# An expert layer on one Trainium2 core: 128 tokens by fetched rows instead of 64, the dense part 384 wide instead of 448

## The chip, the cores and the metric

The kernel runs on one core of a Trainium2 chip, as one program launched once. The metric is the time on the device in microseconds (us). Five engines of the core appear: TensorE (PE, with its weight loads as PEld), VectorE (DVE), ScalarE (ACT), GpSimd (POOL) and SyncE (SP), which here only issues DMAs. All DMAs of the core share 16 DMA engines.

## The reference, cut to what matters

Two transformer blocks run over 512 tokens of width 1024. The first block has sliding-window attention (blocks of 128 tokens; the first block has no block before it, so its masked scores against it become zero weights), a pooling branch, and then an expert layer with 16384 experts. Only these two parts are touched:

```python
kp = jnp.pad(k, ((0,0),(BLOCK,0),(0,0),(0,0)))          # zeros ahead of the first block
mask = (rel >= 0) & (rel < WINDOW) & (kpos[None, :] >= 0)
sc = jnp.where(mask, sc, NEG_INF)                       # softmax over window and sink
...
idx = jnp.take_along_axis(cidx, fi, axis=-1)            # 8 heads x 16 experts for each token
g = jax.nn.softmax(fv, axis=-1)
a = jax.nn.gelu(jnp.einsum('chkd,cd->chk', u_tab[idx], xc))
y = jnp.einsum('chk,chkd->cd', g * a, v_tab[idx])
```

The second block (a recurrent mixer, a feed-forward layer, an embedding gate) is the same before and after.

## The kernel before

Tensors lie with their 1024 channels in 8 chunks of 128 partitions and the 512 tokens along the free dimension. Every large product is made in two parts: each 128x1024 weight tile is loaded raw from memory (512 KB, `Cursor.load`, L143, issued by SP), rounded to a high part by ACT (`high`, L152), and its low part is raw minus high (`low`, L160, on POOL, or on DVE in two stages of the expert layer). `product` (L258 to L260) then issues three matmuls for each 128x128 piece, so a tile costs 24 matmuls. Two raw tiles and two split tiles are held (`RAW = SPLIT = 2`): a raw load waits until the low part of the tile two before it is made, and a rounding waits until TensorE has used the tile two before it.

**Tokens are divided.** The first `GT = 64` tokens take the experts by fetched rows: their 64 x 128 choices fill 64 lists of 128 row numbers, and for each list POOL gathers 128 rows of 4 KB (`Rows.gather`, L1342), first from U, then from V, into a ring of 4. `dot` (L1356, DVE) multiplies fetched U rows with the inputs, `activate` (ACT) and `weigh` (DVE) turn the sums into coefficients, and `add_rows` (L1378, DVE) adds the scaled V rows. The other `TD = 448` tokens are dense: they are multiplied with all experts, 128 tiles of U and 128 tiles of V, with matmuls 448 wide, and a table with the weight of every expert for each dense token zeroes what a token did not choose.

The expert layer runs in this order, hand-written, with the same tile order on every engine:

1. Keys are ranked (`RankKeys`), 16 tiles 512 wide; then PE turns the 64 inputs into rows (`turn_inputs`, L1300: 32 matmuls, of two records each in the trace).
2. The CH stage: 4 turns of 10 U tiles (`up`); beside them DVE chooses the experts of 128 tokens (`Choose.vector`), and at the end of each turn PE transposes the choices. POOL makes the low parts.
3. The table stage: 4 turns of 18 tiles, that is 8 blocks of 9 U tiles, one block of table for `TB = 56` tokens. A step makes 4 tokens: DVE compares (L1207) and weights (L1211) one-hot vectors, PE multiplies them (L1104, 4 matmuls 128 wide), ACT copies the bank to `table_stage`. After a block SP stores it (L1022, 3584 KB). From here on DVE makes the low parts and one `dot` after each of the first 64 tiles. After each U tile ACT takes the activation function (L1157), and SP stores the activations in memory.
4. END: the last 16 U tiles; `activate` stands after tile 1 on ACT, and DVE's `weigh` after the low part of tile 15.
5. The V stage: 128 tiles (`down`). For each, DVE multiplies the loaded activations with the table twice (L1249 to the rounded form, L1250 in full), subtracts (L1252), then makes the low part of a weight tile and adds about one V row list in two tiles. Its first multiplication waits until PE has used the tile two before it. At the end PE adds the row sums (`add_halves`, 8 matmuls).

SP's order for a V tile is the raw weight load (waits for DVE's low part), then the load of the activations four tiles on (waits for the coefficients of this tile), then in half of the tiles two loads of the table.

In attention (`attention`) there are 32 steps of two heads by 128 tokens; each makes scores against two blocks (L819), a softmax on DVE and ACT, four transposes (L846), and the products with the values (L859); between them stand the matmuls of the gates. For the first 8 steps one of the two blocks is zeros.

## Time and profile before

| | us |
|---|---|
| median of 3 runs | 2929.7 (2925.7 to 2933.84) |
| the profiled execution | 2927.18 |
| its span | 2925.4 |
| TensorE's granted clock, mean | 0.971 of 2.4 GHz |

The stages in the trace, in us from the start of the span: attention 127 to 279; CH 519 to 721; table stage 730 to 1176; END 1176 to 1254; V stage 1254 to 1886; after that come a short norm and the second block. In a row of stretches each engine's busy time is followed by the count of its instructions in brackets, then come TensorE's granted clock as a share of full speed, the busy share of the 16 DMA engines and the bytes moved. A line of groups gives total busy time and the mean of one instruction, and behind the bar the idle time before them with what ended it. "Landing" is the time from a DMA's issue until its last byte is reported.

### The profile page before, as it was taken

The numbers are of one execution on the slowest core, as the hardware profiler recorded it, in microseconds if no ns is written. First come the engines' busy times: TensorE is split into PE (matmuls) and PEld (weight loads), VectorE is DVE, ScalarE is ACT, GpSimd is POOL, SyncE is SP. The second block draws the span as 40 slices with busy tenths as digits, with TensorE's granted clock in tenths as the row PEclk, the third lists the DMA queues.
The fourth block names the chain that finished last, engine by engine and source line by source line (L and its number), as shares of the span: only waits on it lengthen the run. The fifth ranks groups of instructions, "written<-read, shape, count | busy, mean of one in ns | idle before, by whom it ended". The sixth has DMA issues, their size and how long they took to land. (4 is left out here: it accounts for less than half of the span.)

```text
span 2925.4 us, 47950 instructions
## 1 busy us (share of the span) xinstructions
PE 2746.0 (94%) x18360; PEld 2380.5 (81%) x18360; DVE 1717.0 (59%) x2968; ACT 1044.1 (36%) x1635; POOL 820.3 (28%) x560
## 2 busy tenths in 40 slices
PE   6999989999999999999999999889799788999997
PEld 4766768889999999989999999767699675888775
DVE  1254349976888886267777777646566644333115
ACT  3366333444333333322222222355334344333233
POOL 2622333455111110001111110133444232444442
PEclk9999999999999999999999999999999988999998
DMA  3211222445777876667777777323922001222221
GB/s 115 93 53 54 84 92 83 126 153 166 261 260 254 298 262 216 233 220 259 258 263 262 261 264 245 115 87 107 301 52 58 17 15 58 100 93 98 103 94 65
DMA packets 191757, 453.37 MB, mean 155 GB/s; under 512 B 57344, under 2 KB 106624, under 8 KB 190336
## 3 DMA queue, kind: packets, MB, share of 16 engines
q1 hardware_dynamic: 173184, 384.30, 38.8%
q0 software_dynamic: 18432, 67.12, 6.7%
q8 instruction: 98, 1.61, 0.2%
q14 instruction: 43, 0.35, 0.0%
HBM read 375.85 MB, written 75.50 MB: 154 GB/s over the span
## 5 line engine op out<-in xcount | busy, mean ns | idle before, releaser
L152 ACT ACTIVATE weights_high<-weights_raw 128x1024 fp32r<-128x1024 f32 x433 | 458.8, 1060 | 1488.7 <-PE psum L260 1435.5
L160 POOL TENSOR_TENSOR weights_low<-weights_raw,weights_high 128x1024 fp32r<-128x1024 f32 x219 | 539.0, 2461 | 852.4 <-ACT weights_high L152 852.4
L258 PE MATMUL psum<-expert_in_high,weights_high 128*128 128x448 f32 (+1 forms) x1152 | 433.8, 377 | 6.7 <-DVE expert_in_low L353 4.9
L260 PE MATMUL psum<-expert_in_high,weights_low 128*128 128x448 f32 (+1 forms) x1152 | 424.8, 369 | 0.0
L259 PE MATMUL psum<-expert_in_low,weights_high 128*128 128x448 f32 (+1 forms) x1152 | 424.7, 369 | 0.0
L258 PE MATMUL psum<-coefficients_high,weights_high 128*128 128x448 f32 x1024 | 376.3, 368 | 4.5 <-DVE coefficients_low L1252 4.5
L260 PE MATMUL psum<-coefficients_high,weights_low 128*128 128x448 f32 x1024 | 375.4, 367 | 0.0
L259 PE MATMUL psum<-coefficients_low,weights_high 128*128 128x448 f32 x1024 | 375.3, 366 | 0.0
L160 DVE TENSOR_TENSOR weights_low<-weights_raw,weights_high 128x1024 fp32r<-128x1024 f32 x214 | 261.3, 1221 | 141.1 <-ACT weights_high L152 140.7
L258 PEld LDWEIGHTS psum<-expert_in_high,weights_high 128*128 128x128 f32 x1152 | 217.0, 188 | 30.8 <-issue 5.7
L1342 POOL DMA_INDIRECT expert_rows<-in_weights,row_numbers x64 | 60.0, 937 | 638.9 <-DVE s_by_token_then_row_sums L1378 478.9
L260 PEld LDWEIGHTS psum<-expert_in_high,weights_low 128*128 128x128 f32 x1152 | 216.8, 188 | 21.2
L259 PEld LDWEIGHTS psum<-expert_in_low,weights_high 128*128 128x128 f32 x1152 | 217.2, 189 | 18.3
L258 PE MATMUL psum<-mix_in_high,weights_high 128*128 128x512 f32 x456 | 187.9, 412 | 29.7 <-POOL weights_low L115 14.8
L258 PEld LDWEIGHTS psum<-coefficients_high,weights_high 128*128 128x128 f32 x1024 | 193.4, 189 | 20.1 <-issue 4.9
L259 PEld LDWEIGHTS psum<-coefficients_low,weights_high 128*128 128x128 f32 x1024 | 193.4, 189 | 15.2
L260 PEld LDWEIGHTS psum<-coefficients_high,weights_low 128*128 128x128 f32 x1024 | 193.2, 189 | 15.4
L259 PE MATMUL psum<-mix_in_low,weights_high 128*128 128x512 f32 x456 | 180.1, 395 | 0.0
L260 PE MATMUL psum<-mix_in_high,weights_low 128*128 128x512 f32 x456 | 179.8, 394 | 0.0
L1249 DVE TENSOR_TENSOR coefficients_high<-activation_in,table_group 128x448 fp32r<-128x448 f32 x128 | 80.1, 626 | 168.5 <-PE psum L260 168.5
L1342 POOL DMA_INDIRECT expert_rows<-in_u_rows,row_numbers x64 | 72.3, 1129 | 308.7 <-DVE row_coefficients L1356 307.5
L258 PE MATMUL psum<-ffn_in_high,weights_high 128*128 128x512 f32 x352 | 138.4, 393 | 4.4 <-DVE ffn_in_low L353 4.3
(399 smaller groups left out, 5025.4 us busy)
## 6 DMA issues: line engine op xcount, KB each, us to landing
weights_raw<-in_weights SPq DMA_DIRECT2D x435, 512.0 KB, 3.8
expert_activations<-expert_activation SPq DMA_DIRECT2D x128, 224.0 KB, 4.6
coefficient_table<-table_stage SPq DMA_DIRECT2D x8, 3584.0 KB, 14.4
table_group<-coefficient_table SPq DMA_DIRECT2D x128, 224.0 KB, 4.4
activation_in<-expert_activations SPq DMA_DIRECT2D x128, 224.0 KB, 3.9
a_and_kk_then_chunks<-scan_vectors SPq DMA_DIRECT2D x8, 768.0 KB, 6.4
scan_vectors<-scan_stage SPq DMA_DIRECT2D x4, 1280.0 KB, 7.0
scan_vectors<-scan_stage SPq DMA_DIRECT2D x4, 1024.0 KB, 6.5
```

What stands on the lines that cost most here:

```text
L152: act.activation(d.hi[:, m % SPLIT, :], d.raw[:, m % RAW, :], ACT.Copy).then_inc(d.high, 1)
L160: pool.tensor_tensor(d.lo[:, m % SPLIT, :], d.raw[:, m % RAW, :], d.hi[:, m % SPLIT, :].bitcast(F32), ALU.subtract).then_inc(d.split, 1)
L258: pe.matmul(acc, w[0][:, cols], x[0], start=start, stop=False)
L259: pe.matmul(acc, w[0][:, cols], x[1], start=False, stop=False)
L260: return pe.matmul(acc, w[1][:, cols], x[0], start=False, stop=stop)
L1249: dve.tensor_tensor(by_block(co[0][:, o, :]), by_block(tile), gt, ALU.mult).then_inc(ex.part, 1)
L1342: pool.indirect_dma_start(self.ring[:, n % self.R, :], None, self.v_rows if table else self.u_rows, bass.IndirectOffsetOnAxis(ap=self.inde ...
```

## The change

`GT` becomes 128 and `TD` 384, so dense matmuls of the expert layer are 384 wide; the table is made in 8 blocks of 48 tokens, with 12 steps each (96 in all instead of 112), and its stores are 3072 KB. There are 128 row lists of U and 128 of V, in two groups of 64 tokens; U's come at 5 for every 4 tiles of the table stage (90), then 3 for each tile of END (38), and V's over 116 tiles of the V stage, from its fifth on. `turn_inputs` has 64 matmuls, `turn_choices` 12 instead of 6, and the final addition 16 instead of 8. `activate` moves on ACT behind END, behind the first two roundings of coefficients, and `weigh` to DVE's fifth V tile. In the V stage DVE multiplies once, a tile ahead; ACT rounds the product; DVE subtracts. SP issues the activation load ahead of the raw weight load. In attention's first 8 steps the block of zeros is left out, and so are two clearings on POOL. The core of the diff:

```diff
-GT = 64
+GT = 128
 TD = T - GT
-TB = 56
+TB = 48
...
+        def blocks(n):
+            return range(0 if n >= QC else 1, 2)
+
+        def seen(n):
+            return slice(blocks(n)[0] * P, 2 * P)
...
-    TBL, TBS = 4, 18
+    TBL, TBS, BLK = 2, 36, 4
...
                 def tiles16(ii, last):
                     for j in range(16):
-                        w.load(sp, ii, j, 16)
                         if not (last and j >= 16 - ex.AR):
                             sp.wait_ge(ex.coef, ii * 16 + (j + 1))
                             sp.dma_start(a_in[:, j % ex.AR, :],
                                          ACTS[bass.ds(ii * 16 + (j + ex.AR), 1)].rearrange("o p t -> p (o t)")
                                          ).then_inc(ex.a_in[j % ex.AR], 16)
+                        w.load(sp, ii, j, 16)
                         par, step = 1 - j // GI8, j % GI8
                         if step < NTB // 2 and not (last and par == 0):
                             for b in (2 * step, 2 * step + 1):
...
                 for j in range(ex.END):
                     up(0, 0, END0 + j, j)
-                    if j == 1:
-                        rows.activate(act)
                 w.advance(ex.END)
-                w.run(act, w.high, ex.ut // 16 - 1, 16)
+
+                def rounded(ii, j):
+                    o = j % ex.CR
+                    act.wait_ge(ex.part, ii * 16 + (j + 1))
+                    act.wait_ge(dense.used, ii * 16 + (w.slots + j + 1 - ex.CR))
+                    act.activation(co[0][:, o, :], a_in[:, j % ex.AR, :], ACT.Copy).then_inc(ex.high, 1)
+
+                for j in range(ex.CR):
+                    rounded(0, j)
+                rows.activate(act)
+                with act.Fori(0, ex.ut // 16 - 1) as ii:
+                    for j in range(16):
+                        w.high(act, ii, j, 16)
+                        rounded(ii, j + ex.CR)
+                w.advance(ex.ut - 16)
+                end = ex.ut // 16 - 1
                 for j in range(16 - SPLIT):
                     w.high(act, 0, j, 16)
+                    act.wait_ge(ex.part, end * 16 + (j + ex.CR + 1))
+                    act.wait_ge(dense.used, w.slots + j + 1)
+                    act.activation(co[0][:, j % ex.CR, :], a_in[:, (j + ex.CR) % ex.AR, :], ACT.Copy).then_inc(ex.high, 1)
...
                             w.low(dve, 0, j, END0 - TABLE0)
                             for _, _, n in table_steps(i, par, q):
                                 if n + ex.RING < steps:
                                     onehots(n + ex.RING)
-                            if j < rows.N:
-                                rows.dot(dve, j)
+                            for s in range(5 * j // 4, 5 * (j + 1) // 4):
+                                rows.dot(dve, s)
                 w.advance(ex.TBL * ex.TBS)
+                dots = 5 * ex.TBL * ex.TBS // 4
                 for j in range(ex.END):
                     w.low(dve, 0, j, ex.END)
-                    if j == ex.END - 1:
-                        rows.weigh(dve)
+                    for s in range(dots + 3 * j, min(dots + 3 * j + 3, rows.N)):
+                        rows.dot(dve, s)
...
-                for n in range(ex.ut):
+                def multiply(n):
                     ii, j = n // 16, n % 16
-                    par, r, o = j // GI8, j % ex.AR, j % ex.CR
+                    par, r = j // GI8, j % ex.AR
                     if j % GI8 == 0:
                         dve.wait_ge(ex.g_in[par], ii * (16 * NTB) + 16 * NTB)
                     dve.wait_ge(ex.a_in[r], ii * (16 * 16 // ex.AR) + (16 * (j // ex.AR) + 16))
-                    dve.wait_ge(dense.used, w.slots + n + 1 - ex.CR)
-                    tile, gt = a_in[:, r, :], g[:, par, :, j % GI8, :]
-                    dve.tensor_tensor(by_block(co[0][:, o, :]), by_block(tile), gt, ALU.mult).then_inc(ex.part, 1)
-                    dve.tensor_tensor(by_block(tile), by_block(tile), gt, ALU.mult).then_inc(ex.part, 1)
-                    dve.wait_ge(ex.part, 2 * n + 2)
-                    dve.tensor_tensor(co[1][:, o, :], tile, co[0][:, o, :].bitcast(F32), ALU.subtract).then_inc(ex.coef, 1)
+                    dve.tensor_tensor(by_block(a_in[:, r, :]), by_block(a_in[:, r, :]), g[:, par, :, j % GI8, :],
+                                      ALU.mult).then_inc(ex.part, 1)
+
+                multiply(0)
+                for n in range(ex.ut):
+                    if n + 1 < ex.ut:
+                        multiply(n + 1)
+                    o = n % ex.CR
+                    dve.wait_ge(ex.high, n + 1)
+                    dve.tensor_tensor(co[1][:, o, :], a_in[:, n % ex.AR, :], co[0][:, o, :].bitcast(F32),
+                                      ALU.subtract).then_inc(ex.coef, 1)
                     if n >= SPLIT:
                         w.low(dve, 0, n - SPLIT, ex.ut)
                     rows.add_rows(dve, n, ex.ut)
...
-    R, N = 4, P // 2
-    HALVES = (slice(0, GT), slice(GT, 2 * GT))
+    R = 4
+    GROUPS = ((0, 64), (64, 64))
+    N = sum(width for _, width in GROUPS)
...
     def turn_inputs(self, pe):
 
-        for c in range(DC):
-            for r in self.HALVES:
-                for part in range(2):
-                    mm = pe.matmul(self.k.ps[r, 2 + c // 4, c % 4 * P:(c % 4 + 1) * P], self.xn[part][:, c, 0:GT].bitcast(F32),
-                                   self.k.consts("ident"), start=part == 0, stop=part == 1)
-            if c % 4 == 3:
+        for g, (first, width) in enumerate(self.GROUPS):
+            for half in range(2):
+                n = 2 * g + half
+                if n == 3:
+                    pe.wait_ge(self.copied, 1)
+                for c in range(4 * half, 4 * half + 4):
+                    for part in range(2):
+                        tokens = self.xn[part][:, c, first:first + width].bitcast(F32)
+                        for p in range(0, P, width):
+                            mm = pe.matmul(self.k.ps[p:p + width, self.bank(n), c % 4 * P:(c % 4 + 1) * P], tokens,
+                                           self.k.consts("ident"), start=part == 0, stop=part == 1)
                 mm.then_inc(self.turned, 1)
...
     def add_rows(self, dve, n, tiles):
 
-        last = tiles - 8
-        for s in range(n * self.N // last, min((n + 1) * self.N // last, self.N)):
+        first, count = 4, tiles - 12
+        if n == first:
+            self.weigh(dve)
+        n = max(n - first, -1)
+        for s in range(max(n, 0) * self.N // count, min((n + 1) * self.N // count, self.N)):
+            g = self.group(s)
             dve.wait_ge(self.weighed if s == 0 else self.used, 1 if s == 0 else self.N + s)
-            row, by = self.row(dve, self.N + s), self.coef[:, s:s + 1]
-            if s == 0:
-                ins = dve.tensor_scalar(self.x[:, :], row, by, None, ALU.mult)
+            row, by, x = self.row(dve, self.N + s), self.coef[:, s:s + 1], self.x[:, g, :]
+            if s == self.GROUPS[g][0]:
+                ins = dve.tensor_scalar(x, row, by, None, ALU.mult)
             else:
-                ins = dve.scalar_tensor_tensor(out=self.x[:, :], in0=row, scalar=by, in1=self.x[:, :], op0=ALU.mult, op1=ALU.add)
+                ins = dve.scalar_tensor_tensor(out=x, in0=row, scalar=by, in1=x, op0=ALU.mult, op1=ALU.add)
             ins.then_inc(self.used, 1)
...
+    def add_parts(self, pe, c):
+
+        for g, (first, width) in enumerate(self.GROUPS):
+            pe.matmul(self.k.ps[:, c, first:first + width], self.x[:, g, c * P:(c + 1) * P], self.k.consts("eye2"),
+                      start=False, stop=False)
```

## Rows read from the trace of the kernel before

**Rows 1.** The page, part 1: TensorE's busy time, share of the span, instructions.
```profile
PE 2746.0 (94%) x18360; PEld 2380.5 (81%) x18360; DVE 1717.0 (59%) x2968; ACT 1044.1 (36%) x1635; POOL 820.3 (28%) x560
```

**Rows 2.** Stretches: length, busy (x) of PE, PEld, DVE, ACT, POOL; PEclk, DMA share, GB/s.
```profile
127.00:279.00 152.00, 147.59 (x861) 102.05 (x860) 83.67 (x186) 93.12 (x278) 48.50 (x24) 0.99 0.16 56
519.00:721.00 202.00, 198.38 (x976) 181.18 (x973) 159.05 (x392) 84.94 (x113) 102.21 (x40) 1.00 0.47 145
730.00:1176.00 446.00, 446.00 (x2600) 420.65 (x2599) 358.10 (x417) 160.49 (x253) 69.74 (x65) 1.00 0.74 257
1176.00:1254.00 78.00, 74.03 (x366) 68.28 (x364) 21.13 (x20) 24.00 (x33) 0.00 (x0) 0.99 0.68 232
1254.00:1886.00 632.00, 628.27 (x3088) 581.72 (x3088) 453.66 (x581) 141.35 (x137) 60.64 (x64) 0.99 0.70 244
```

**Rows 3.** Stretches without a stall: 512 wide in the feed-forward, 448 wide in the V stage.
```profile
2470.00:2700.00 230.00, 230.00 (x1015) 190.26 (x1016) 79.74 (x64) 84.11 (x85) 100.57 (x42) 1.00 0.27 94
1330.00:1800.00 470.00, 470.00 (x2321) 435.53 (x2320) 344.42 (x440) 103.00 (x97) 47.78 (x51) 1.00 0.74 259
```

**Rows 4.** Timeline of PEld (start us, us): a table product's loads, then one V stage load.
```profile
751.28 0.86 PEld L1104 LDWEIGHTS psum<-st_and_second_key_onehot,second_key_weighted 128*128 128x128 f32 x7
...
1400.09 0.19 PEld L258 LDWEIGHTS psum<-coefficients_high,weights_high 128*128 128x128 f32 x1
```

**Rows 5.** Timeline of one V tile: weight rounded, its low part, next load's issue, next rounding.
```profile
1402.91 1.07 ACT L152 ACTIVATE weights_high<-weights_raw 128x1024 fp32r<-128x1024 f32 x1 [3.80 <-PE psum L260]
...
1404.72 1.22 DVE L160 TENSOR_TENSOR weights_low<-weights_raw,weights_high 128x1024 fp32r<-128x1024 f32 x1
...
1406.11 0.33 SPq L143 DMA_DIRECT2D weights_raw<-in_weights  x1
...
1407.78 1.06 ACT L152 ACTIVATE weights_high<-weights_raw 128x1024 fp32r<-128x1024 f32 x1 [3.80 <-PE psum L260]
```

**Rows 6.** Stretches of saturated DMA: around a table store, and within the V stage.
```profile
780.00:792.00 12.00, 12.00 (x72) 11.32 (x71) 9.84 (x12) 4.44 (x7) 1.87 (x2) 1.00 1.01 400
1396.00:1401.00 5.00, 5.00 (x26) 4.63 (x26) 4.25 (x6) 1.06 (x1) 0.94 (x1) 1.00 1.00 362
```

**Rows 7.** By tile: issue to landing of expert_rows, then of weights_raw.
```profile
DMA to landing us min/median/max: 4.0/5.5/12.4
...
DMA to landing us min/median/max: 3.3/3.8/12.3
```

**Rows 8.** Timeline of attention, step by step on PE: value products, then transposes.
```profile
152.09 0.66 PE L859 MATMUL psum<-probabilities_transposed,values_by_token 128*64 128x128 f32 x8
...
152.73 0.66 PE L846 MATMUL psum<-tables,probabilities 128*128 128x128 f32 x4
```

**Rows 9.** Timeline of PE: the first and the last of 16 groups that turn inputs.
```profile
515.41 0.45 PE L1300 MATMUL psum<-tables,expert_in_high 128*64 128x128 f32 x4
...
518.74 0.44 PE L1300 MATMUL psum<-tables,expert_in_low 128*64 128x128 f32 x4
```

**Rows 10.** Groups by line: shapes and count | busy us, mean ns | idle before.
```profile
L160 DVE TENSOR_TENSOR weights_low<-weights_raw,weights_high 128x1024 fp32r<-128x1024 f32 x214 | 261.3, 1221 | 141.1 <-ACT weights_high L152 140.7
L1207 DVE TENSOR_TENSOR st_and_second_key_onehot<-tables,choices 128x1024 f32<-128x1024 f32 x112 | 136.4, 1218 | 0.0
L1211 DVE TENSOR_TENSOR second_key_weighted<-st_and_second_key_onehot,choices 128x512 f32<-128x512 f32 x112 | 77.5, 692 | 3.8
L1356 DVE CUSTOM_DVE_ANT_0 expert_rows<-expert_rows,s_by_token_then_row_sums 128x1024 f32<-128x1024 f32 x64 | 77.9, 1218 | 0.0
L1378 DVE SCALAR_TENSOR_TENSOR s_by_token_then_row_sums<-expert_rows,row_coefficients,s_by_token_then_row_sums 128x1024 f32<-128x1024 f32 x63 | 80.6, 1279 | 0.0
L1249 DVE TENSOR_TENSOR coefficients_high<-activation_in,table_group 128x448 fp32r<-128x448 f32 x128 | 80.1, 626 | 168.5 <-PE psum L260 168.5
```

**Rows 11.** Timeline behind a table store: raw weight load on SP, the rounding that waited.
```profile
785.46 0.35 SPq L143 DMA_DIRECT2D weights_raw<-in_weights  x1
...
797.17 1.06 ACT L152 ACTIVATE weights_high<-weights_raw 128x1024 fp32r<-128x1024 f32 x1 [5.98 <-DMA weights_raw<-in_weights]
```

101 lines of the change are left out of this document (53 added, 48 removed).

## The prediction

> **What bounds the kernel now.** I read the page's busy times first, then busy times by stretch, then the timeline of single tiles, then DMA. TensorE is busy 94% of the span [rows 1], but its matmul records overlap, so this alone proves nothing; the stretches do. In the table stage it is busy 446.0 of 446 us and in the V stage 628.3 of 632, at full clock, while DVE has 358 and 454 and no other engine more than a third [rows 2]. A V tile is 24 matmuls, and two roundings of weights, which wait for TensorE, lie 4.87 us apart [rows 5]: 0.203 us a matmul. So from 519 to 1886 us the kernel runs at the pace of dense matmuls. The reader should see a second resource there: DMA moves 244 to 257 GB/s at shares of 0.70 to 0.74 [rows 2], and for whole stretches it is full, at 400 GB/s around a table store and at 362 inside the V stage [rows 6]. The change takes matmul columns away and pays with fetched rows, so it moves load from the first resource to the second.
>
> **The price of a narrower matmul.** Without stalls 512 columns cost 230/1015 = 0.2266 us and 448 cost 470/2321 = 0.2025 [rows 3]: 64 columns are worth 0.0241. No 384-wide matmul of this kind stands in the trace. Its bounds are 0.1784 (the same step again) and 0.2025 (no gain, if the weight load sets the pace: its record takes 0.19 [rows 4]). I take 0.1784, because seven weight loads of the table product fit into 0.86 us [rows 4], (0.86 - 0.19)/6 = 0.112 apart: the record is longer than the time for which the unit is held. A tile then saves 24 x 0.0241 = 0.58 us and takes 4.29.
>
> The Trainium skill (Perfetto Trace Analysis, Identifying the Most-Contended Engine) says the opposite of that step: nearness to the limit is to be read from the busy share of weight loads, not of matmuls. That share is 436 of 470 us in the V stage [rows 3], 93%, which would leave nothing to gain from fewer columns. It is rival 3.
>
> **Part by part**, against the profiled execution (2927.2 us; span 2925.4). The median of the three runs, 2929.7, is 2.5 above it.
>
> *Attention.* In 8 of 32 steps half of the scores, transposes and value products goes. The value products take 152.73 - 152.09 = 0.64 us a step and the transposes 0.66 [rows 8]; the scores, four records as well, I price like the transposes. Half of 1.96 is 0.98, times 8 is 7.8; since neighbouring records overlap a little, -7. The bounds are 0 (DVE and ACT pace the first steps; but their pieces shrink too) and -11. The two clearings on POOL lie at the start under the first loads: 0.
>
> *Turning inputs.* 16 groups lie (518.74 - 515.41)/15 = 0.22 apart [rows 9]; 16 more, on TensorE's path: +3.6. The extra choices turned and the eight extra final additions are few and short: +0.5.
>
> *CH stage.* 40 tiles x 0.58 = -23. The cover to watch is DVE's choosing: 159 us in four turns [rows 2], 39.8 a turn, against 42.9 for ten tiles. It fits, but in the first turn DVE starts after TensorE: +2, bounds 0 and +12 (3 a turn).
>
> *Table stage.* 72 tiles x 0.58 = -42. A step of table product costs (446 - 72 x 4.87)/112 = 0.85; 16 fewer are -14. A tile is then 4.29 + 96/72 x 0.85 = 5.43 instead of 6.19. DVE per tile, by the means of [rows 10]: before 1.22 + 1.56 x 1.91 + 0.89 x 1.22 = 5.28, which is 4.97 in busy time (358/72); after 1.22 + 1.33 x 1.91 + 1.25 x 1.22 = 5.29, so again 4.98. Its work stays and its time shrinks, from 80% to 92%: close, not the bound. A raw load issued behind a table store waited 797.17 - 785.46 = 11.7 us [rows 11] instead of 3.8 [rows 7]. Two tiles of 6.19 hid that; two of 5.43 are 1.5 less, while the store is 0.5 MB shorter (1.3 us at 400 GB/s) and 40% more rows a tile share the way. Bounds 0 and 3 us for each of 8 stores; I take +10.
>
> *END.* Its 16 tiles save 9, but rows now come at three a tile. Bytes: 16 x (0.52 + 0.20) for weights and activations, 42 row lists x 0.52 (four of V ahead), 12 x 0.20 for the first tables and activations: 35.9 MB. At 380 GB/s, between the two full stretches of [rows 6], that is 94 us against 78 before [rows 2]: +16. Bounds -9 (all hidden) and +42 (300 GB/s). The ring of four rows alone (5.5 landing [rows 7] + 1.2 dot, over four) is 1.7 a row, 64 us for 38, so DMA binds first.
>
> *V stage.* 128 x 0.58 = -74. DVE drops from three passes over the coefficients (0.63 each [rows 10]) to two of about 0.56; with the low part 1.22 and 1.1 row lists at 1.28 it has 3.75 of 4.29 us. The added ACT rounding of about 0.5 lies behind the weight's 1.07 [rows 5] and ahead of DVE's subtraction and low part: 1.07 + 0.5 + 0.56 + 1.22 + 0.2 of signals = 3.5, hidden while it stays below 4.29. The next raw load goes out about there, lands 3.8 later [rows 7], at 7.4, and is wanted after two tiles, 8.6. Before it was 3.2 [rows 5] + 3.8 = 7.0 of 9.7. So 2.7 us of cover become 1.2: landing may grow to 5.0, no further. The activation load now leaves a tile earlier, ahead of the weight on SP; behind it waits only the raw load, and on the coefficients of a tile that are made before the low part in question, so it costs nothing.
> Bytes per tile are 0.52 + 0.39 + 1.10 x 0.52 = 1.50 MB, 349 GB/s over 4.29 us. Half of the tiles carry two table loads, 1.69 MB: at 362 GB/s [rows 6] these take 4.68, 0.39 too long, 64 x 0.39 = 25 if nothing is smoothed by the lighter tiles, 0 if all is. I take +18, nearer the upper end since the ring is full at times already, and +2 for tiles with two row lists on DVE: -54.
>
> The Trainium skill (DMA: Bandwidth & Descriptors, Measured) gives 341 GB/s for transfers of 1 MB and less for smaller ones. By that the heavy tiles would take 4.96 and the stage would lose 43 instead of 18; the trace has 362 with transfers of half a megabyte.
>
> **Sum.** -7 + 3.6 + 0.5 - 23 + 2 - 42 - 14 + 10 + 16 - 54 = -108: 2819 for the profiled execution, 2822 beside the median.
>
> **Rivals.**
> 1. *DMA never binds* (loads smooth out; nothing falls behind). Then the +10, the 25 of END above its 69, and 18 of V go away: -161, 2769. For it: mean demand in V, 333 GB/s over the whole stage, is below 362. Against it: END's demand of three rows a tile, 2.3 MB in 4.29 us, cannot be met.
> 2. *DMA binds harder*, sustaining 300 GB/s: V 182 MB is 608 us (+30), table stage 124 MB 414 (+13), END 120 (+26): 2891. For it: small cover for raw loads, DVE taking rows in order so that one late row holds back a low part. Landing already reaches 12 us [rows 7].
> 3. *Weight loads set the pace*, so no tile gets shorter: -7 + 4 + 2 - 14 + 16 + 2 = +3, 2933. For it: the weight-load share of 93% [rows 3], with records of 0.19 in a spacing of 0.203 [rows 4, 5]. Against it: the 24 ns step from 512 to 448 and the loads 0.112 apart [rows 3, 4].
> 4. *Slower.* Row fetches take more from DMA than matmuls give: V, table and END together move 343 MB and took 1156 us. With -24 from the rest the change loses from 343/(1156 + 24 + 9) = 288 GB/s downward; at 270 it is 1270 us, +90: 3020. Against it: bytes over share in [rows 2] is 257/0.74 = 347.
> 5. *The rows do not relieve the dense part*: excluded, the width is a slice.
>
> **From numbers to chances.** Forecast (2790 to 2855) 0.62; rival 1 0.12; rival 2 0.15; rival 3 0.05; rival 4 0.04; 0.02 between. The range 2770 to 2875 takes in rival 1 and the near half of rival 2, and so the bounds of the stores, END and V. A difference under 0.3% (9 us) cannot be told from none. Faster 0.90, same 0.05, slower 0.05.
>
> **What would show it.** In the changed kernel: V stage and CH spacing of 0.178 us a matmul in stretches without stalls; table stage about 400 us, END about 94 with TensorE waiting for DVE's low parts and DVE for rows; V stage near 578 with DMA share above 0.85 and a raw landing above 4 us; attention 7 shorter; nothing changed from the end of the V stage on. A spacing of 0.20, or raw landings beyond 5 us through the whole V stage, would make it wrong.

## The result, and the profile after

The changed kernel takes 2888.35 us (median of 4 runs, 2883.65 to 2894.22) beside 2931.77 for the kernel before in the same session (4 runs): a ratio of 0.985, 95% interval 0.983 to 0.988. It is faster by 1.5%, but by 43 us and not by 108, and 13 us outside the range. The profiled execution took 2883.65 (span 2881.6, before 2925.4). Two executions of kernels further down (one of 3112.48 us with the rows at an even pace, one of 4295.0 us with three edits) ran at a granted clock of 0.83 and 0.56 and are left out of every median and ratio.

The page's part 1 after, beside [rows 1]: TensorE has lost 142 us of busy time and is busy 90% instead of 94%. Less work fills a smaller share of a span that shrank by 44 us only.

```profile
PE 2604.2 (90%) x18276; PEld 2308.0 (80%) x18276; DVE 1742.3 (60%) x3000; ACT 1082.2 (38%) x1749; POOL 1038.0 (36%) x686
```

Busy time by stretch after, beside [rows 2], columns as there; attention, CH, table stage, END and V stage:

```profile
127.00:276.00 149.00, 144.87 (x826) 99.80 (x825) 85.57 (x190) 93.46 (x282) 48.19 (x24) 1.00 0.18 57
519.00:697.00 178.00, 170.09 (x960) 164.37 (x958) 158.73 (x347) 80.96 (x111) 115.99 (x40) 1.00 0.55 155
703.00:1106.00 403.00, 385.07 (x2446) 383.24 (x2445) 354.81 (x435) 148.90 (x236) 143.20 (x90) 0.99 0.85 297
1106.00:1222.00 116.00, 82.64 (x406) 80.28 (x404) 66.33 (x96) 25.71 (x35) 55.13 (x41) 0.85 0.95 343
1226.00:1842.00 616.00, 567.22 (x3103) 550.18 (x3102) 434.65 (x516) 193.07 (x263) 140.88 (x128) 0.97 0.86 292
```

Before, TensorE was busy 446 of 446 us in the table stage and 628 of 632 in the V stage. Now it idles 18, 33 and 49 us in the last three stretches. Yet DMA carries only 292 GB/s at a share of 0.86 in the V stage: it is not full on average there. The medians from issue to landing over the whole run show the price of the load; the last line is the activation load before:

```profile
weights_raw<-in_weights SPq DMA_DIRECT2D x435, 512.0 KB, 4.0
activation_in<-expert_activations SPq DMA_DIRECT2D x128, 192.0 KB, 5.4
expert_rows<-in_u_rows,row_numbers POOLq DMA_INDIRECT x128, 7.6
expert_rows<-in_weights,row_numbers POOLq DMA_INDIRECT x128, 6.4
...
activation_in<-expert_activations SPq DMA_DIRECT2D x128, 224.0 KB, 3.9
```

The stages were also measured between fixed marks, the same in all kernels: CH and the table stage between the activation functions of their first and last tiles, END from the last one of the table stage to its own last, V from its first to its last matmul. "V", "table stage" and "END" with a time below mean these. Each is one profiled execution; parts that no edit touched differ by up to 6 us between the kernels (the first U tile ends at 521.5 to 527.8 us, CH takes 172.9 to 178.6), so a difference of that size between two stages is not told from none.

| us | before | forecast change | after | change |
|---|---|---|---|---|
| start to the first U tile's end | 526.7 | -3 | 523.0 | -4 |
| CH | 193.2 | -21 | 173.0 | -20 |
| table stage | 443.8 | -46 | 404.7 | -39 |
| END | 79.7 | +16 | 114.8 | +35 |
| V stage | 631.4 | -54 | 616.6 | -15 |
| all the rest | 1050.6 | 0 | 1049.5 | -1 |

Two steps carry 58 of the 64 us by which the trace misses the sum: V 39 us and END 19; the table stage has 7 more. What DVE, ACT and TensorE waited for in the V stage (engine, line, tile <- what ended the wait: us in total, times, longest):

```profile
ACT weights_high L152 <- DMA weights_raw<-in_weights: 241.9, 72, 5.5
DVE activation_in L1269 <- DMA activation_in<-expert_activations: 123.2, 75, 4.8
PEld psum L258 <- DVE weights_low L160: 52.2, 45, 4.0
PE psum L258 <- DVE weights_low L160: 44.7, 36, 3.7
```

TensorE waits for DVE's low part. DVE in turn waited 123 us for activation loads, which no line of the forecast had. That is the clue the experiments follow.

### The profile page after: what moved, and what is told of

The parts are those of the page before. It is cut to its first block and busy times, and to the rows that moved or that the text cites. A ratio compares the mean times of both kernels' runs of the same rounds, so it can differ in the third digit from the quotient of the medians.

```text
span 2881.6 us, 48184 instructions
## 1 busy us (share of the span) xinstructions
PE 2604.2 (90%) x18276; PEld 2308.0 (80%) x18276; DVE 1742.3 (60%) x3000; ACT 1082.2 (38%) x1749; POOL 1038.0 (36%) x686
## 5 line engine op out<-in xcount | busy, mean ns | idle before, releaser
L258 PE MATMUL psum<-expert_in_high,weights_high 128*128 128x384 f32 (+1 forms) x1152 | 410.7, 356 | 59.0 <-DVE weights_low L160 45.2
L258 PE MATMUL psum<-coefficients_high,weights_high 128*128 128x384 f32 x1024 | 355.7, 347 | 51.3 <-DVE weights_low L160 44.7
L259 PE MATMUL psum<-expert_in_low,weights_high 128*128 128x384 f32 (+1 forms) x1152 | 399.8, 347 | 0.0
L260 PE MATMUL psum<-expert_in_high,weights_low 128*128 128x384 f32 (+1 forms) x1152 | 399.8, 347 | 0.0
L259 PE MATMUL psum<-coefficients_low,weights_high 128*128 128x384 f32 x1024 | 349.3, 341 | 0.0
L260 PE MATMUL psum<-coefficients_high,weights_low 128*128 128x384 f32 x1024 | 349.2, 341 | 0.0
L1387 POOL DMA_INDIRECT expert_rows<-in_u_rows,row_numbers x128 | 196.1, 1532 | 313.2 <-DVE row_coefficients L1401 298.5
L1387 POOL DMA_INDIRECT expert_rows<-in_weights,row_numbers x128 | 141.4, 1105 | 433.8 <-DVE s_by_token_then_row_sums L1427 392.4
L1401 DVE CUSTOM_DVE_ANT_0 expert_rows<-expert_rows,s_by_token_then_row_sums 128x1024 f32<-128x1024 f32 x128 | 154.2, 1220 | 34.6 <-DMA expert_rows<-in_u_rows,row_numbers 34.4
L1427 DVE SCALAR_TENSOR_TENSOR s_by_token_then_row_sums<-expert_rows,row_coefficients,s_by_token_then_row_sums 128x1024 f32<-128x1024 f32 x126 | 161.2, 1280 | 0.4
```

The source lines that it names most:

```text
L258: pe.matmul(acc, w[0][:, cols], x[0], start=start, stop=False)
L259: pe.matmul(acc, w[0][:, cols], x[1], start=False, stop=False)
L260: return pe.matmul(acc, w[1][:, cols], x[0], start=False, stop=stop)
L1387: pool.indirect_dma_start(self.ring[:, n % self.R, :], None, self.v_rows if table else self.u_rows, bass.IndirectOffsetOnAxis(ap=self.inde ...
L1401: dve.tensor_tensor_reduce(row, row, self.x[:, self.group(s), :], 1.0, 0.0, ALU.mult, ALU.add, self.coef[:, s:s + 1]).then_inc(self.used, 1)
L1427: ins = dve.scalar_tensor_tensor(out=x, in0=row, scalar=by, in1=x, op0=ALU.mult, op1=ALU.add)
```

## The experiments

Each is one edit, or a sum of edits, on the changed kernel; diffs are against it. Ratios are to the kernel before, run on the same chip in the same session (its medians there: 2923.7 to 2928.3). The changed kernel's own ratio is 0.985.

### Is it the row bytes, or the order on SP?

The first kernel loads only the first half of each fetched row; the other half of each row is left out of the computation.

```diff
...
-            pool.indirect_dma_start(self.ring[:, n % self.R, :], None, self.v_rows if table else self.u_rows,
+            pool.indirect_dma_start(self.ring[:, n % self.R, 0:D // 2], None,
+                                    (self.v_rows if table else self.u_rows).rearrange('n (h d) -> (n h) d', h=2),
...
```

> The changed kernel, with 2 KB fetched for each row instead of 4 KB; the other half of each ring slot stays zero, so the row sums are not the reference's. The number of fetches, DVE's work and the order stay. Theory: the bytes of the rows hold the stages back, by share and by landing time. V stage carries 150 MB instead of 182 and should fall from 616 us to about 545 (TensorE's own 533 and a little), END from 112 to about 80, table stage from 405 to about 395; total 2888 to about 2790. Rival (the number of fetches, POOL's issue or DVE taking rows in order holds them back): total within 10 us of 2888.

Measured: 2802.85 us (0.958, 0.955 to 0.962). V 570.3, table stage 391.1, END 92.9. In the V stage:

```profile
1192.00:1768.00 576.00, 555.58 (x3109) 541.91 (x3108) 437.19 (x522) 195.80 (x269) 147.47 (x128) 0.99 0.79 258
DVE activation_in L1269 <- DMA activation_in<-expert_activations: 78.6, 65, 3.0
```

Row bytes matter, 46 us of V, but less than was expected of them (about 71, to 545). With DMA at 258 GB/s and a share of 0.79, not far above the load of before (244, 0.70 in [rows 2]), V is still 37 us above TensorE's 533 (128 tiles of 4.16 us, as measured below), and DVE still waits 79 us for activations. Fullness alone is not the cause.

The second kernel puts the raw weight load ahead of the activation load again, as in the kernel before.

```diff
                     for j in range(16):
+                        w.load(sp, ii, j, 16)
                         if not (last and j >= 16 - ex.AR):
...
-                        w.load(sp, ii, j, 16)
```

> The changed kernel, with SP's old order in the V stage: raw weight load first, then the activation load. Theory A (the activations ahead of the weight delay the raw loads, for which 72 roundings wait): V stage shorter by 10 to 30 us. Theory B (the advance helps: with a landing of 5.4 us the activations are late without it): V stage longer by 10 to 40 us. Neither (both loads only share the same full channel): within 5 us.

Measured: 3111.43 us (1.064, 1.062 to 1.067); V 843.1, the largest effect of all runs: theory B's direction, and 227 us longer where it said 10 to 40. The timeline (start us, us) of one of its tiles and of one of the changed kernel, SP's loads and DVE's multiplication. Old order:

```profile
1601.03 0.33 SPq L143 DMA_DIRECT2D weights_raw<-in_weights  x1
1601.59 0.33 SPq L1050 DMA_DIRECT2D activation_in<-expert_activations  x1
...
1605.14 0.56 DVE L1269 TENSOR_TENSOR activation_in<-activation_in,table_group 128x384 f32<-128x384 f32 x1 [3.08 <-DMA activation_in<-expert_activations]
```

Changed kernel:

```profile
1524.52 0.33 SPq L143 DMA_DIRECT2D weights_raw<-in_weights  x1
1525.05 0.33 SPq L1049 DMA_DIRECT2D activation_in<-expert_activations  x1
...
1530.30 0.56 DVE L1269 TENSOR_TENSOR activation_in<-activation_in,table_group 128x384 f32<-128x384 f32 x1 [1.12 <-DMA activation_in<-expert_activations]
```

SP stands at the raw load until a low part is made (L143 waits for it), and whatever is behind it on SP leaves with it. With the old order DVE multiplies these very activations at the start of its next tile: it had been ready at 1602.06 (1605.14 - 3.08), half a microsecond after the load's issue, and then waits for the whole landing, in each of 124 tiles, 394.7 us in all. In the changed kernel it wants them one tile later, 4.1 us after the issue (1530.30 - 1.12 - 1525.05), and the load took 5.25. So the order on SP is worth one tile of lead, and one tile of lead (4.16 us) is less than a landing of 5.4. In the kernel before, with the old order and the multiplication in the tile itself, the lead was one tile too, but of 4.87 us, against a landing of 3.9, and no wait for activations was among its waits.

### How much lead, and who used it up?

The activations of tile j+5 instead of j+4 ahead of the weight load:

```diff
+                sp.wait_ge(ex.coef, 1)
+                sp.dma_start(a_in[:, 0, :], ACTS[ex.AR]).then_inc(ex.a_in[0], 16)
...
-                            sp.wait_ge(ex.coef, ii * 16 + (j + 1))
-                            sp.dma_start(a_in[:, j % ex.AR, :],
-                                         ACTS[bass.ds(ii * 16 + (j + ex.AR), 1)].rearrange("o p t -> p (o t)")
+                            sp.wait_ge(ex.coef, ii * 16 + (j + 2))
+                            sp.dma_start(a_in[:, (j + 1) % ex.AR, :],
+                                         ACTS[bass.ds(ii * 16 + (j + 1 + ex.AR), 1)].rearrange("o p t -> p (o t)")
```

> Only SP's order in the V stage changes: the load of the activations of tile j+5 goes out ahead of the raw weight load of tile j+4, where the changed kernel sends the activations of tile j+4; that is one whole tile earlier, into a slot that is free by then. Bytes and work are the same. Theory A (the stage loses to too little cover: DVE multiplies one tile ahead, and its 123 us of waits for activations come from loads that have 5.5 us for a landing of 5.4): these waits fall below 30 us, a part of them comes back as waits for raw weights, V falls from 616.6 to 580 to 595, the kernel to about 2860. Theory B (the DMA engines are simply full at some 300 GB/s, and each wait only marks where the shortage shows): the waits move whole to the raw weights (242 to about 350), V stays at 608 to 617, the kernel at 2880 to 2890.

Measured: 2858.09 us (0.976, 0.973 to 0.979); V 592.7, so theory A. What ended the waits of the engines before their operations on `activation_in`:

```profile
  ACT coefficients_high L1195: 96.5, 63
  DMA table_group<-coefficient_table: 23.4, 13
```

No wait for activations is left in it. Waits of ACT for raw weights did not grow, against what was expected of this run (240.6 us, 241.9 in the changed kernel).

The same lead in the old order, by asking behind the raw load for the activations two tiles further on:

```diff
...
+                        w.load(sp, ii, j, 16)
-                            sp.wait_ge(ex.coef, ii * 16 + (j + 1))
-                            sp.dma_start(a_in[:, j % ex.AR, :],
+                            sp.wait_ge(ex.coef, ii * 16 + (j + 3))
+                            sp.dma_start(a_in[:, (j + 2) % ex.AR, :],
...
-                        w.load(sp, ii, j, 16)
```

> SP's order in the V stage as in the kernel before, the raw weight load first; but the activations that follow it are those of two tiles further on than the kernel before asked for (tile j+6 behind the raw load of tile j+4). Bytes and work are those of the changed kernel. Theory A (what counts is how many tiles ahead of DVE's multiplication the load goes out; the order of the two loads on SP does not matter by itself): the lead is two tiles and V comes out as with the load asked for one tile earlier ahead of the weight, 588 to 598 us, the kernel near 2858. Theory B (the activation load must stand ahead of the weight load, for instance because the weight's wait holds it back): V over 610, up to the 843 that the old order gave with the old lead.

Measured: 2867.42 us (0.978, 0.974 to 0.982); V 593.6, the same as the run above. The order on SP by itself is worth nothing that can be seen; the tiles of lead count: 0, 1 and 2 tiles gave V 843, 617 and 593.

What had used the lead up? DVE multiplying one tile ahead was the suspect; this kernel multiplies in the tile itself, with SP's order of the changed kernel:

```diff
-                multiply(0)
                 for n in range(ex.ut):
-                    if n + 1 < ex.ut:
-                        multiply(n + 1)
+                    multiply(n)
```

> One edit on the changed kernel: DVE multiplies the activations of tile n in tile n again, not in tile n-1. SP's order, ACT's rounding and the rows stay. The activation load then has one tile more before it is wanted. Theory A (the multiplication moved ahead is what used up the lead of the activation load): DVE's waits for activations fall from 123 us to below 20, and instead DVE waits some 0.8 us a tile for ACT's rounding between multiplication and subtraction, of which most lies in time it has to spare; V 590 to 605. Theory B (the waits for activations are a sign of the full DMA engines, the lead does not matter): they stay above 80 us and V is 617 or more, since a wait for ACT is added.

Measured: 2849.79 us (0.973, 0.969 to 0.976); V 584.7, better than theory A's 590 to 605. The same view there (the first row is DVE waiting for ACT, the second ACT for DVE), and ACT's waits for raw weights:

```profile
  ACT coefficients_high L1192: 110.3, 99
  DVE activation_in L1269: 26.7, 33
  ACT coefficients_high L1207: 20.2, 14
```
```profile
ACT weights_high L152 <- DMA weights_raw<-in_weights: 291.2, 101, 4.9
```

The wait for activations is gone, and a wait of 130 us for ACT's rounding has taken its place. It costs less, which fits the time that DVE has to spare: it is busy 437 of 591 us. Taking one line of the change back gives 32 of V's 39 missing microseconds.

### What else a low part waits for

DVE's low part of the weight ahead of the subtraction of the coefficients, which waits for ACT:

```diff
+                    if n >= SPLIT:
+                        w.low(dve, 0, n - SPLIT, ex.ut)
                     dve.wait_ge(ex.high, n + 1)
...
-                    if n >= SPLIT:
-                        w.low(dve, 0, n - SPLIT, ex.ut)
```

> The changed kernel, with DVE making the low part of the weight before the subtraction of the coefficients in the V stage, so that the next raw load goes out about 1 us earlier; same bytes, same work. Theory cover (the V stage is held back by the short time between a raw load's issue and its use): V stage 616 to about 570. Theory throughput (DMA is full): V stage within 8 us of 616, with roundings that wait as long as before.

Measured: 2861.48 us (0.978, 0.975 to 0.980); V 595.0. SP's next raw load hangs on the low part, and it now leaves 0.6 us earlier in each tile (the subtraction's 0.55): ACT's waits for raw weights fall from 241.9 us to 151.6, DVE's for activations only to 108.1. This is a second loss, of the raw load's cover, beside the first. V stands about midway between the two theories (570 and 616): the cover was half of what was expected of it.

### Table stage and END

The U rows at an even pace, 16 per 11 tiles, instead of 5 per 4 and then 3 per tile:

```diff
-                            for s in range(5 * j // 4, 5 * (j + 1) // 4):
+                            for s in range(16 * j // 11, 16 * (j + 1) // 11):
...
-                    for s in range(dots + 3 * j, min(dots + 3 * j + 3, rows.N)):
+                    for s in range(16 * (tiles0 + j) // 11, 16 * (tiles0 + j + 1) // 11):
```

> The changed kernel, with the 128 U rows spread evenly, 16 for every 11 of the 88 tiles, instead of 5 for 4 in the table stage and 3 for 1 in END. Theory: END's burst is what costs 112 us for work that needs 67 on TensorE; END falls to about 80 and the table stage grows by 5 to 10: total -20 to -30. Rival (table stage and END together are limited by bytes, which stay): total within 8 us.

Measured: 2876.30 us (0.984, 0.981 to 0.987), in total not to be told from the changed kernel, as the rival said. END fell by 27 us to 88.0, the table stage grew by 12 to 416.3: the rows were carried over, and part of the gain with them. The two stages together are 15 us shorter; 8 of these are lost again in the trace in CH and ahead of it, which the edit does not touch.

The table store in four parts, the last three behind the raw loads of the next tiles:

```diff
-                            sp.dma_start(dram["table"][i * ex.BLK + par], stage[:, par % 2, :, :]).then_inc(ex.t_stored[par % 2], 16)
+                            store_part(i * ex.BLK + par, par % 2, 0)
+                        elif j >= BLOCK_S and j % BLOCK_S < 4:
+                            par = j // BLOCK_S - 1
+                            store_part(i * ex.BLK + par, par % 2, j % BLOCK_S + 1)
...
```

> Each 3072 KB store of a table block is cut into four of 768 KB: the first goes where the whole one went, the others behind the raw loads of the next tiles. Bytes are the same. Theory A (the table stage loses its 23 us over TensorE's 382 to the bursts of the eight stores, behind which a raw load waits): the stage falls from 404.7 to 385 to 392, gelu periods of 10 to 12 us behind the stores vanish, the kernel gains 12 to 20 us. Theory B (the stage is short of DMA throughout, 297 GB/s at a share of 0.85): the stage stays within 4 us of 404.7. END and V stay as they are, 115 and 617, in both.

Measured: 2869.44 us (0.981, 0.978 to 0.984). Table stage 386.3, inside theory A's 385 to 392, with 4 us left above TensorE's 382 (an estimate: 72 x 4.16 + 96 x 0.85); END 108.8. The stretch, and beside it that of the changed kernel with the same marks:

```profile
712.00:1098.00 386.00, 380.83 (x2461) 379.88 (x2460) 354.85 (x436) 149.40 (x237) 140.23 (x90) 1.00 0.89 312
```
```profile
705.00:1110.00 405.00, 387.07 (x2462) 385.24 (x2461) 354.71 (x435) 150.07 (x237) 142.30 (x89) 0.99 0.85 298
```

The same bytes at a higher rate: the 18 us were the bursts of eight stores, 2.3 us each. That they came from raw loads behind the stores is the reading of [rows 11]; the run shows only that splitting the stores takes them away.

### Do the losses add up, and what is left?

Three edits together (activations a tile earlier, low part first, even rows), then with the split store as a fourth. The diffs are those above.

> Three edits at once on the changed kernel: activations asked for one tile earlier, the low part of a weight tile ahead of the subtraction on DVE, and the U rows spread evenly over the table stage and END (16 per 11 tiles). Alone the last two gave 27 and 11 us. Theory A (each of them removes a wait of its own kind): V 570 to 580, table and END together 504, the kernel 2830 to 2845. Theory B (V is bounded by DMA at 316 GB/s, which the low part ahead already reached in its 595 us): V 590 to 595, the kernel 2850 to 2855.

Measured: 2822.08 us (0.964, 0.961 to 0.967); V 565.5, below both theories; table stage 418.7 and END 89.5.

> The three edits together with the table store in four parts. The store alone took the table stage from 404.7 to 386.3 and END from 115 to 109; the three edits alone had 418.7 and 89.5 there, 508.2 in all, and V 565.5. Theory A (bursts and average load are separate losses and add up): table stage and END together 482 to 494, V as before, the kernel 2803 to 2815. Theory B (with 42% more rows per tile in the table stage the DMA engines are full there at 312 GB/s, so that smoothing the stores gains less): together 498 to 508, the kernel 2818 to 2828.

Measured: 2805.42 us (0.957, 0.952 to 0.961); V 565.6, table stage 395.6, END 91.0, together 486.6: theory A, they add up. V is the same as with three edits.

```profile
706.00:1108.00 402.00, 392.36 (x2507) 390.21 (x2506) 378.07 (x473) 152.33 (x240) 174.19 (x107) 0.99 0.90 322
1202.00:1766.00 564.00, 544.49 (x3091) 538.47 (x3092) 430.99 (x517) 191.96 (x262) 142.16 (x128) 0.99 0.90 321
```

Both stages now carry 321 to 322 GB/s on average at a share of 0.90. Is that what is left? The four edits with half rows (the other half left out of the result, as above):

> The four edits, and only half of each fetched row is loaded (2 KB of 4 KB); the other half of each row is left out of the result. DVE's work, the number of rows and all waits are the same. This asks what is left of V's distance to TensorE's own time: 565.5 against 533. Theory A (it is DMA: 319 GB/s at a share of 0.90): V falls to 533 to 542, table stage to 380 to 385, END to 67 to 72, the kernel 2745 to 2765. Theory B (it is the chain of DVE and ACT inside a tile): V stays above 555, the kernel above 2780.

Measured: 2761.21 us (0.942, 0.938 to 0.947); V 542.6, table stage 386.7, END 78.3. V is a hair outside theory A's 533 to 542 and far from B's 555; table stage and END fell less than A said (380 to 385, 67 to 72). Of the 33 us by which V stood above TensorE's 533, 23 were row bytes. The other 10 are not in the tiles: by TensorE's first matmuls the tiles from the ninth to the 116th are 4.16 us long on average, so they lie at the two ends of the stage. V's floor is thus taken as 543.

```profile
1181.00:1724.00 543.00, 536.99 (x3096) 536.12 (x3094) 435.33 (x518) 195.10 (x267) 147.60 (x130) 1.00 0.81 270
```

Four edits and the multiplication in its own tile:

> The four edits, and DVE's multiplication in its own tile: multiplication, low part of the weight, subtraction. The low part (1.22 us) covers ACT's rounding of the product (0.5 us and signals). Theory A (multiplying ahead brings nothing once the low part stands between): V within 6 us of 565.6, the kernel 2800 to 2812. Theory B (the chain from the activation to the coefficients' low part becomes the bound when it starts a tile later): TensorE's waits for the coefficients' low part, 22.8 us with the four edits, grow beyond 40, V above 575.

Measured: 2798.36 us (0.955, 0.952 to 0.959), the lowest time of a kernel that leaves nothing out, 3.1% below the changed one by the two ratios (0.9552/0.9853). It is not to be told from the four edits alone (0.957, 0.952 to 0.961). V 562.1, theory A; table stage 396.8, END 90.0.

```profile
1198.00:1760.00 562.00, 543.33 (x3086) 537.72 (x3087) 432.26 (x520) 195.84 (x264) 143.96 (x129) 0.99 0.91 323
```

### The uneven tiles of the V stage

Stretches of 20 us within the V stage of the changed kernel. Half of its tiles carry two table loads:

```profile
1600.00:1620.00 20.00, 19.83 (x113) 19.47 (x114) 17.94 (x22) 6.57 (x10) 6.69 (x6) 1.00 0.89 291
1620.00:1640.00 20.00, 17.39 (x91) 17.07 (x90) 12.23 (x15) 5.89 (x8) 3.75 (x4) 0.91 0.96 337
1640.00:1660.00 20.00, 20.00 (x117) 19.76 (x116) 17.38 (x20) 5.93 (x9) 6.88 (x5) 1.00 0.88 287
1660.00:1680.00 20.00, 16.45 (x84) 15.81 (x84) 11.75 (x16) 5.86 (x8) 3.75 (x4) 0.91 0.95 338
```

Stretches without a stall alternate with stretches in which DMA is at 0.95 to 0.96 and TensorE idles 3 us. That looks like the forecast's term: the heavy tiles bind. So the table loads were spread, one with each tile, three tiles ahead of their old places:

```diff
...
-                        par, step = 1 - j // GI8, j % GI8
-                        if step < NTB // 2 and not (last and par == 0):
-                            for b in (2 * step, 2 * step + 1):
-                                sp.dma_start(g[:, par, b, :, :], table_in[ii * 2 + (j // GI8 + 1), :, b]).then_inc(ex.g_in[par], 16)
+                        ahead, b = divmod(j + 11, NTB)
+                        if not (last and ahead > 1):
+                            sp.dma_start(g[:, ahead % 2, b, :, :], table_in[ii * 2 + ahead, :, b]).then_inc(ex.g_in[ahead % 2], 16)
```

> One edit on the changed kernel: the eight table loads of a group go out one with each V tile, three tiles ahead of where they went, instead of two with each of four tiles and none with the other four. Bytes are the same. Theory A (a tile with two table loads, 1.69 MB, binds on DMA, as the forecast's term of 18 us said, and the late tiles are those): V falls from 616.6 to 595 to 605. Theory B (the losses come from the short lead of the activation load, wherever the table loads stand): V stays within 5 us of 616.6.

Measured: 2924.59 us (0.999, 0.997 to 1.001); V 659.3. Neither theory: V is 43 us longer than in the changed kernel, and the whole gain of the change is gone. Its waits in the V stage:

```profile
DVE activation_in L1271 <- DMA activation_in<-expert_activations: 81.0, 59, 5.1
DVE activation_in L1271 <- DMA table_group<-coefficient_table: 78.8, 15, 8.5
```

The last table load of a group now leaves one tile later than before, and DVE, which multiplies a tile ahead, stands 5.3 us for it at each of 15 groups. It is the same fault again, a load whose lead had been used up. The edit was made without counting that, and so it does not test the term.

The same edit on the fastest kernel, where the multiplication is in its own tile and the lead is there:

> The four edits, the multiplication in its own tile, and the table loads one with each tile. The same kernel without the last edit had V 562.1, 2798.4 in all, with tiles of 3.9 to 4.8 us. Theory A (uneven demand is what is left): V 545 to 555, all tiles within 0.2 us of each other, the kernel 2782 to 2793. Theory B (mean demand is, at 323 GB/s and a share of 0.91): V stays within 4 us of 562, the kernel at 2795 to 2801.

Measured: 2803.03 us (0.958, 0.956 to 0.961), against 2798.36 without it (0.955, 0.952 to 0.959): no difference, and V 559.5: theory B's stage, and 2 us over its range for the kernel. By itself this does not settle what is left of V, 19 us over its floor of 543, because the tiles became only a little more alike: nine in ten are now below 4.8 us instead of 5.1, the shortest 4.16 in both. The middle of the V stage of the kernel without this edit does settle most of it:

```profile
1564.00:1714.00 150.00, 145.70 (x831) 143.51 (x830) 120.81 (x143) 52.31 (x71) 40.28 (x36) 1.00 0.98 353
```

DMA is full there, 353 GB/s at a share of 0.98, while a tile's 1.50 MB (the prediction's count) every 4.16 us would be 361 (an estimate). The mean of 323 over the stage takes in its ends, where no rows are fetched. So with every lead restored the mean demand is at the limit; whether unevenness adds something to it is not shown. That the late tiles with table loads in the changed kernel were in part a matter of leads, since SP issues two table loads between a raw load and the next activation load, is argued and was not tested.

### Fewer rows

96 tokens by fetched rows and a dense part 416 wide (`GT = 96`, `TB = 52`, groups of 64 and 32 tokens), with the three edits; 12 rows per 11 tiles.

```diff
-GT = 128
+GT = 96
-TB = 48
+TB = 52
...
-    GROUPS = ((0, 64), (64, 64))
+    GROUPS = ((0, 64), (64, 32))
```

> The three edits, with 96 tokens by fetched rows instead of 128 and a dense part 416 wide. Between the measured 0.1735 us a matmul at 384 and 0.2025 at 448, 416 should cost 0.188, a tile 4.51 us: TensorE alone then needs 180 in CH, 72 x 4.51 + 104 x 0.85 = 413 in the table stage, 72 in END, 577 in V. Theory A (128 tokens ask for more DMA than there is, and the right amount lies below): every stage lies within 2% of TensorE's time, V 577 to 588, the kernel 2825 to 2840, no slower than with 128 tokens and the same edits. Theory B (with cover restored the DMA engines carry 128 tokens): 96 tokens are 10 to 30 us slower than the 128 with the same edits.

Measured: 2859.11 us (0.978, 0.975 to 0.981), 37 us slower than 128 tokens with the same edits (2822.08): theory B, by 7 us more than its range. V in the profile:

```profile
1228.00:1819.00 591.00, 588.03 (x3115) 582.68 (x3114) 403.65 (x484) 197.69 (x265) 103.00 (x97) 0.99 0.84 283
```

TensorE is the bound again: tiles of 4.52 us, 128 of which are 579, and the ends of the stage; V 592.8. Against 96, 128 tokens were not too many; the schedule around them had been too tight.

## Why the prediction was wrong, point by point

**What bounds the kernel before, and the price of a width: right.** Roundings without a stall stand 4.16 us apart after ([rows 5] has 4.87), 0.1733 us a matmul; forecast 0.1784, bounds 0.1784 and 0.2025.

```profile
1500.92 1.06 ACT L152 ACTIVATE weights_high<-weights_raw 128x1024 fp32r<-128x1024 f32 x1 [2.69 <-PE psum L260]
...
1505.08 1.06 ACT L152 ACTIVATE weights_high<-weights_raw 128x1024 fp32r<-128x1024 f32 x1 [2.69 <-PE psum L260]
```

The value lies outside the lower bound by 3%, to the good: 128 tiles take 533, not 549. This hides part of the miss: the forecast put V 20 us over its TensorE time (632 - 74 = 558, then 578); it came out 74 over the floor of 543. The same 0.12 us a tile, 0.70 saved instead of 0.58, hides 5 us in CH, 9 in the table stage and 2 in END. Rival 3, weight loads as the pace, is ruled out: the spacing fell by 14%, to below the 0.193 us of a load's own record. The records of loads overlap each other, so their busy share says little here. The Trainium skill (Perfetto Trace Analysis, Identifying the Most-Contended Engine) reads nearness to the limit from that share, together with the share of the peak arithmetic rate; the share was 93% in [rows 3], and this case's trace does not bear it out as a measure of what a narrower matmul can save.

**Attention: right.** The value products of the same late step start at 190.22 us before and at 183.81 after: 6.4 against 7.

```profile
183.81 0.66 PE L863 MATMUL psum<-probabilities_transposed,values_by_token 128*64 128x128 f32 x8
```

**Turning inputs, CH: right in number, by luck.** The first U tile ends 4 us earlier (forecast 3), within the spread of that mark. CH lost 20 (21), but at the measured price its tiles should have lost 28, so the stage gave 8 back where +2 was forecast (bounds 0 and 12). In 12 of the 14 later kernels with the same CH it was 177 to 179, a loss of 15 only. Why is not explained.

**Table stage: nearly right, in part by luck.** -39 against -46. The +10 for stores were 18 (the split store took them back), inside the bounds of 0 to 24; the cheaper matmul's 9 us covered that. DVE at 92% (355 of 386 us, with the split store) did not bind.

**END: two terms wrong.** Its bytes left out the last block's store:

```profile
1110.72 0.33 SPq L1027 DMA_DIRECT2D coefficient_table<-table_stage  x1
```

With 3.1 MB the bytes are 39.0 instead of 35.9 MB, and the rate was 343 GB/s at a share of 0.95, not 380: 39.0 MB at 343 GB/s are 114 us, and 115 were measured. The 380 came from two stretches of 5 and 12 us in [rows 6]; neither spoke for 100 us, for which no run had more than 366. With even rows END is 88 to 91 us, 8 to 11 over before instead of 35, and the table stage 12 longer.

**V stage: the step that failed.** The forecast said that the activation load "now leaves a tile earlier" and "costs nothing". It does leave a tile earlier than the old order would let it; but DVE's multiplication was moved a tile ahead, and nothing in the working moved the want with it. So the lead stayed one tile, and it was never computed: 4.16 us. Even a raw load's 3.8 in [rows 7] would have left 0.4 of it; the landing became 5.4, and DVE waited 75 times, 123 us in all. Restoring it gave 24 us (a tile more lead) or 32 (multiplication in its own tile).
The raw load's cover of 1.2 us was computed, "landing may grow to 5.0, no further", and its median in V became 5.0:

```profile
DMA to landing us min/median/max: 3.4/5.0/7.7
```

The working had the threshold and the growing load in neighbouring sentences and did not put them together; 0.6 us more cover (low part first) was worth 22 us. With both repaired V is 562.1, 19 above the floor, and the forecast's terms for DMA and DVE there were 20: that part was of the right size, partly by luck, since the working put it down to the heavy tiles at 362 GB/s and the runs point to mean demand. The last paragraph named "raw landings beyond 5 us through the whole V stage" as a sign of being wrong; their median stood at 5.0, just at the line.

**The rivals.** Rival 2 (DMA sustains 300 GB/s: V 608, table 414, END 120, 2891) came within 3 us of the total and 10 of each stage, with a chance of 0.15. Its number was right and its mechanism in V was not: the changed kernel moves 292 GB/s there because engines wait in turn, and the same bytes went at 323 once the leads were there. A mean rate below the limit is what a latency problem looks like, too. The range ended at 2875 because it took in "the near half" of this rival. One figure of rival 1 does not come out of its rows: V's 182 MB over 578 us are 315 GB/s of mean demand, not 333; the conclusion drawn from it, that this is below 362, stands either way.

## What to carry to other kernels

When a consumer is moved ahead of its old place, compute for each of its loads the lead, from the instruction that lets the queue issue it to the instruction that wants it, in tiles and then in microseconds of the new, shorter tile, and compare it with the landing time under the new load. An edit that shortens the tile shortens every such lead, and an edit that adds bytes lengthens every landing; a schedule that was safe by one microsecond is not safe after both. If total bytes over time stay below what the same engines carry elsewhere, look for a wait in the chain before calling it bandwidth, and make bursts smaller before taking work away.

## What the runs showed of the hardware

- The matmul spacing by width, without stalls: 0.2266 us at 512 and 0.2025 at 448 [rows 3], 0.189 at 416 (588.03/3115), 0.1733 at 384. The last 64 columns were worth 0.029, the 64 before 0.024; the step was not a constant.
- DMA of this mixture (512 KB and 192 KB transfers and lists of 128 rows of 4 KB) carried 321 to 323 GB/s over 400 and 560 us at a share of 0.90 to 0.91, 343 over 116 us at 0.95 (END of the changed kernel), 353 over 150 us at 0.98, and at most 366 over 100 us, with the split store:

```profile
1093.00:1193.00 100.00, 73.95 (x360) 71.34 (x360) 63.98 (x94) 22.12 (x30) 51.38 (x39) 0.85 0.98 366
```

  The 400 of [rows 6] stood for 12 us. The Trainium skill (DMA: Bandwidth & Descriptors, Measured) has 341 GB/s for transfers of 1 MB and less for smaller ones; these transfers are smaller, and this case's traces were above it for 100 to 150 us.
- TensorE's granted clock fell where it idled: 0.91 in the stretches of 20 us with 3 us idle, 1.00 in those without, 0.85 over END, a mean of its two levels, 1.2 and 2.4 GHz. Of the 73 us between the V stage of the changed kernel (616) and that of the four edits with half rows (543), 43 are idle time of TensorE and 30 are busy time, 567 us instead of 537 for the same matmuls, at a granted clock of 0.97 instead of 1.00. So a stall costs more than its own length; how much of the 30 is the clock was not measured by itself.
